# Another hand-written order for the seven step sequences of the second block's RWKV and convolution branch

## What is computed

```python
def conformer_conv(u, conv_w, conv_b, ln_g, ln_b):
    h = u[..., :D_CONV] * jax.nn.sigmoid(u[..., D_CONV:])
    h = lax.conv_general_dilated(h, conv_w[:, None, :], ..., feature_group_count=D_CONV) + conv_b  # 31 taps
    return jax.nn.silu(layer_norm(h, ln_g, ln_b))

def rwkv7_recurrence(r, w, k, v, kk, a):        # 8 heads of 64, one step a token
    def step(S, inp):
        s_kk = jnp.einsum("bhvk,bhk->bhv", S, kk_t)
        S = S * w_t - s_kk[..., None] * (kk_t * a_t) + v_t[..., None] * k_t
        return S, jnp.einsum("bhvk,bhk->bhv", S, r_t)
...
y = jnp.concatenate([y_conv, y_rwkv], axis=-1) @ w_out[i]
x = x + rms_norm(y, g[1])
```

## Time and profile before

| | us |
|---|---|
| median of 3 runs | 1634.03 |
| lowest, highest | 1633.18, 1635.67 |
| the profiled execution, its own time | 1632.09 |
| its span | 1630.2 |
| PE busy in the span | 1574.6 |
| first, second, third stretch (by windows) | 131.1, 118.7, 53.0 |

### The profile page before, as it was taken

One profiled execution on the slowest core, in us unless ns is written; L12 is line 12 of the kernel. 1 busy time (PEld: TensorE's weight loads), 2 busy tenths in 40 slices (PEclk: granted clock), 3 DMA queues, 4 the chain that ended last, 5 costly groups with the idle time before them and its releaser, 6 DMA issues.

```text
span 1630.2 us, 26875 instructions
## 1 busy us (share of the span) xinstructions
PE 1574.6 (97%) x11510; PEld 1298.0 (80%) x11510; DVE 819.4 (50%) x1243; ACT 604.0 (37%) x968; POOL 394.6 (24%) x326
## 2 busy tenths in 40 slices
PE   7999999999999999999999988899999999999997
PEld 7898778778888888888777767779779888888876
DVE  4777533446333333334679977547537332333334
ACT  4444322324323233244455544334345332232222
POOL 3111012022201011024057433023013430330234
PEclk9999999999999999999999988999999999999998
DMA  6325212223222323223321100032121222222211
GB/s 222 118 91 194 77 53 78 78 97 136 103 102 80 104 78 103 102 80 117 129 70 63 53 3 3 29 128 107 52 75 56 104 97 88 100 86 97 102 63 67
DMA packets 29221, 146.03 MB, mean 90 GB/s; under 512 B 3104, under 2 KB 6704, under 8 KB 14128
## 3 DMA queue, kind: packets, MB, share of 16 engines
q1 hardware_dynamic: 29104, 144.33, 24.9%
HBM read 138.03 MB, written 6.29 MB: 89 GB/s over the span
## 4 chain that ended last, share of the span: by engine, by line
PE 79%; DVE 9%; issue 7%; POOL 2%; ACT 2%; DMA 0%; SPq 0%; POOLq 0%; DVEq 0%
PE ps L170 78%; DVE zf L182 3%; DVE wl L182 2%; POOL zf L182 2%; DVE ps L190 1%; ACT zf L176 1%; DVE zf L190 1%; PE ps L173 1%; DVE zr L190 1%; DVE zf L2363 1%; ACT wh L179 0%; POOL tn L182 0%; DMA raw<-in_wstream 0%; ACT zr L179 0%; SPq L193 0%
## 5 line engine op out<-in xcount | busy, mean ns | idle before, releaser
L170 PE MATMUL ps<-zr,wh 128*128 128x512 f32 (+3 forms) x4048 | 1170.3, 376 | 9.9 <-ACT wh L179 5.7
L170 PEld LDWEIGHTS ps<-zr,wh 128*128 128x128 f32 (+1 forms) x4048 | 727.5, 189 | 157.9 <-ACT wh L179 5.7
L170 PE MATMUL ps<-zr,wl 128*128 128x512 f32 (+3 forms) x2024 | 748.6, 372 | 0.0
L182 POOL TENSOR_TENSOR zf<-zf 128x512 f32<-128x512 f32 (+1 forms) x237 | 286.6, 1215 | 765.0 <-ACT zf L176 505.5
L170 PEld LDWEIGHTS ps<-zr,wl 128*128 128x128 f32 (+1 forms) x2024 | 380.8, 189 | 71.7
L182 DVE TENSOR_TENSOR wl<-raw,wh 128x1024 fp32r<-128x1024 f32 (+1 forms) x244 | 305.8, 1292 | 204.2 <-ACT wh L179 204.1
L179 ACT ACTIVATE wh<-raw 128x1024 fp32r<-128x1024 f32 (+1 forms) x244 | 240.7, 1034 | 186.4 <-PE ps L170 185.2
L176 ACT ACTIVATE zf<-zf 128x512 f32<-128x512 f32 (+2 forms) x232 | 127.6, 561 | 370.6 <-DVE zf L182 257.7
L182 DVE TENSOR_TENSOR zf<-ps,zf 128x512 f32<-128x512 f32 (+4 forms) x172 | 98.0, 577 | 162.7 <-PE ps L170 140.8
L170 PE MATMUL ps<-zf 64*64 64x64 f32 (+6 forms) x3768 | 156.2, 247 | 20.9 <-issue 8.9
L170 PEld LDWEIGHTS ps<-zf 64*64 64x64 f32 (+3 forms) x3768 | 120.9, 150 | 59.2 <-issue 38.8
(11 more groups left out here) (81 smaller groups left out, 591.3 us busy)
## 6 DMA issues: line engine op xcount, KB each, us to landing
raw<-in_wstream SPq DMA_DIRECT2D x116, 1024.0 KB, 4.8
zf<-in_xT SPq DMA_DIRECT2D x16, 256.0 KB, 2.7
raw<-in_wstream SPq DMA_DIRECT2D x4, 768.0 KB, 4.4
kv_scratch<-zf SPq DMA_DIRECT2D x8, 256.0 KB, 2.2
x_scratch<-zf SPq DMA_DIRECT2D x8, 256.0 KB, 2.1
zf<-x_scratch SPq DMA_DIRECT2D x8, 256.0 KB, 4.8
out<-zf SPq DMA_DIRECT2D x16, 128.0 KB, 1.7
zf<-in_cu SPq DMA_DIRECT2D x1, 1256.0 KB, 8.9
```

Of the source, the lines that this page charges most:

```text
L170: return self.raw.matmul(out_, l, x, start=start, stop=stop)
L182: return self.raw.tensor_tensor(out_, a, b, o)
```

## The change

Only the 421 letters of `TURNS` differ; `TURNS_2`, all steps and all loops are the same. Every sequence advances as often as before; what changes is which letter stands where, and so how the steps lie between the half tiles and between each other.

```diff
 TURNS = """
-...ppp...pp.p.p.pp.pggggp.pppp.hhggg..ccgghhcccggg.hcccc..gcc.cggghghggghgccccgcc.hcccc.hcggggg.cc.hc.
+...ppp...pp.pp.p.pp..g.gpg.g.gpgcggg.pc.ccpcp.gg.hhccggcg.hgh.ggchch.ghccc.ghccggc.cgccch.hg.ghpppcc
```

More of the change, by code:

```diff
@@ L22 @@
 TURNS = """
[L23 to L27, removed]
+...ppp...pp.pp.p.pp..g.gpg.g.gpgcggg.pc.ccpcp.gg.hhccggcg.hgh.ggchch.ghccc.ghccggc.cgccch.hg.ghpppcc
+g.pgcch.cphgc.chchppcggg.cc.pggcp.hpcgghc.c.pgcp.hg.pcghc.gphcpiiphcggicipgigihccicffiggffpggccpcffc
+cifigifgpiccfpgiciifpfpcfgipifppicfpcpigcipfghifhchiphghppgfffhhcffccfhghfchcgfhpfchhgccccghfcpphfcp
+cfchpphhccfpppfhhppcifihfcihciciifficiifiicffifccoooioifiofiofifofoioifofoifioifffoffooffffofofofofo
+foofooofoooffoooooooo
 """
```

## The result

| us | before | changed |
|---|---|---|
| median of 20 runs | 1633.33 | 1635.32 |
| lowest, highest | 1628.84, 1635.67 | 1630.50, 1641.46 |
| ratio to before, 95% interval | 1 | 1.0019 (1.0010 to 1.0028) |
| profiled execution, its span | 1632.09, 1630.2 | 1634.29, 1632.5 |

The changed kernel is 0.19% slower, some 2 to 3 us, where 4.3 us less were forecast. The time lies in the stated range, the sign is wrong.

A forecast was written before the change was run, and what follows sets the result against it. TensorE, busy 97% of the span, was taken as the bound, so only its waits and half-clock time could be won. Terms -2.3 - 1.7 - 0.9 + 0.6 + 0 = -4.3 us gave 1629.7 against 1634.0, range 1624.5 to 1638.5.

The forecast's parts named there:

- (a): First stretch, third transpose of pair 0: four half tiles ahead of it hide the 2.32 us wait for VectorE, -2.3 us.
- (b): First stretch, behind that transpose: the 3.40 us half-clock window goes with the wait, -1.7 us.
- (c): First stretch, level 3 of pair 0: x 3 no longer waits 0.90 us for VectorE, -0.9 us.
- (d): New waits in the first stretch: only prep.kn 1 short of cover, at most 0.3 us, taken as 0.
- (e): More changes between dense and small steps, 82 instead of 74: four pairs more at 0.14 us, +0.6 us.
- (f): Second stretch: four more taps and new waits cost +3.2 us, fewer waits later repay; taken as 0, ends -5 and +9.5.
- a gain: Rival, second stretch: the 2.40 us wait, its half-clock window and state-step waits go, about -5 more, 1624.7 us; chance 0.20.
- given back: Rival: four waits behind the last p tile cost 3.2 us and nothing repays them, 1632.9 us; chance 0.20.
- Slower: the clock: Rival: waits within 14 us of the last p tile drop the clock, three more windows cost 9.5, 1639.2 us; chance 0.18.

The follow-up runs named there:

- y4_turn_heads: Kernel before with pair 0's third transpose behind one dense half and its first five head steps one or two half tiles later: 1630.50 us, 0.9975.
- e3_turn: Kernel before with only the third transpose of pair 0 and the gates of pair 1 one half tile later: 1637.24 us, 1.0018.
- x2_first_before: Order of the kernel before up to the last p tile, remaining letters behind it in the changed order: 1633.14 us, 1.0000 against before.
- y5_taps_late: Kernel before with four taps moved from the first stretch to behind the last p tile, nothing else: 1632.50 us, 0.9995.
- y1_level_back: Changed kernel with pair 0's last level put back ahead of the last dense half: 1634.23 us, 0.9998 against the kernel before.
- y2_level_late: Kernel before with x 5 and tz 4 of pair 0 moved behind the last dense half: 1637.15 us, 1.0022.
- a_look1: A further single trace of the changed kernel, nothing altered: 1639.12 us.
- z4_both: First stretch of z1_taps_off_level with the changed order behind the last p tile: 1631.72 us, 0.9993 against the kernel before.
- z1_taps_off_level: y4_turn_heads with two taps moved from ahead of level z 2 of pair 0 to behind x 3: 1631.40 us, 0.9984 against the kernel before.

## Why the prediction was wrong, step by step

(a) and (b) were right in mechanism and size: -2.3 and -1.7 at their place, in the changed kernel (no wait at the third transpose, granted clock 1.00 in the first stretch of all five traces) and alone in `y4_turn_heads` (-4.1 us by the ratio, -4.0 in its first stretch). `e3_turn` shows that the step behind the transpose needs cover as well; in the changed kernel the head steps come two half tiles behind it.

(c) was right at `x` 3 (between it and the `z` it needs stand a dense half and the gate product, no small step), but in the sum the new waits of (d) outweigh it.

(d) failed. I took 0 and bounded it by 0.3, after looking for steps with too little dense work between themselves and what they need. The changed kernel has four new waits in the first stretch: 1.05 us at `prep.gates` 1, and at `z` 1, `tz` 2 and `prep.vmm` 1:

```profile
860.86 0.67 PE L170 MATMUL ps<-zf 64*64 64x32 f32 x32 [0.37 <-DVE zf L182]
...
886.45 0.69 PE L170 MATMUL ps<-cf_sb,zf 64*64 64x64 f32 x32 [0.58 <-DVE zf L182]
899.02 1.10 PE L170 MATMUL ps<-zf,cf_sb 128*128 128x512 f32 x2 [0.53 <-DVE zf L190]
```

Together they are 2.5 us. All end on VectorE, whose queue there I had not walked. For the longest, these are VectorE's rows and then PE's:

```profile
870.13 3.12 DVE L190 SCALAR_TENSOR_TENSOR ps<-zf,vecs_sb,ps 128x512 f32<-128x512 f32 x4
873.16 3.44 DVE L182 TENSOR_TENSOR wl<-raw,wh 128x1024 fp32r<-128x1024 f32 x2
876.53 0.74 DVE L182 TENSOR_TENSOR zf<-ps,cu_sb 128x256 f32<-128x256 f32 x2
...
876.99 1.45 PE L170 MATMUL ps<-zf 64*128 64x512 f32 x4 [1.05 <-DVE zf L182]
```

`prep.gates` 1 takes the PSUM banks of `qt` 0, and VectorE empties them (876.53) only behind four taps and the split of a weight unit, 6.6 us of work. A dense half (2.8 us) between two steps is cover only if VectorE reaches its part within it, and a bank that comes round is a need like any other. With -4.9 for (a) to (c), +2.5 here, 59 records less (about -1.0) and the one pair of (e) that lies there (+0.1), the first stretch comes to -3.3 against -3.1 measured.

(e) can't be read by itself. Of its four pairs one lies in the first stretch and three in the third. PE is idle 0.4 us in the third, which takes 5.2 us more with 111 records that the other stretches have less; the 3 us named for them and three pairs of 0.14 were 1.8 too little. This is no loss of the whole by itself: `x2_first_before` has the same third stretch (58.0 us) and the time of the kernel before.

(f) failed, in its walk. VectorE's side of it held: the level was put at 5.1 us behind the last `p` tile and ended at 922.07 - 917.05 = 5.0. PE's side did not: I had PE "through at 4.8" and counted waits from `pk` on. PE was standing at `x` 5 and `tz` 4 for 1.53 and 1.75 us already, since each waits for VectorE's work on the step before it, so `pk` started at 9.5 instead of 6.5 and `fin.y` 0 at 36.0 instead of 31.6. The four taps, which I made the cause, cost nothing that the runs can tell from 0 (`y5_taps_late`); the level that lost its dense half costs 3.4 to 3.6 us (`y1_level_back`, `y2_level_late`), and it stood in the diff as two `h` less ahead of the last stop (19 for 21). What spoke for a gain, fewer waits at state steps and the 2.40 us wait, came in part (that wait is 0.70 and 1.58 us in two places now) and is worth nothing in the runs.

The sum as measured: -4.1 for (a) and (b), +2.5 less 0.9 for (d) and (c), +3.5 for the level, 0 for the second order: +1.0, where the runs give +2 to +3. Intervals of 1.6 to 2.6 us a term cover the difference. The traces show where it lies: up to `fin.y` 0 the five of the changed kernel take 36.0 to 40.0 us, 37.8 in the mean, for 31.7 before: +6.1, of which the first stretch gives back 3.1; behind `fin.y` 0 the means are 140.5 and 140.0. The trace with 36.0 has no half-clock window ahead of 940 us, the other four have; how much of the further 1.8 us is the clock's no run isolates.

The rivals: *given back* named the right outcome with the wrong cause. *Slower: the clock* was right in its mechanism, that waits within 14 us of the last `p` tile are followed by a fall of a clock that was full there (in six of the seven traces with the bare level), and the long runs lie at its 1639.2 (`a_look1` has its signs, 123.9 us in the second stretch and 41.0 at half clock). But the clock does not fall in each run, and the mean half-clock time of the two kernels is the same: by the means, the first stretch's 3.4 us went behind the last `p` tile. The Trainium skill, "TensorE: Matmul & The Clock Gate", section "What's actually happening", says that the window over which the gate judges activity runs free and is not reset when a kernel starts, so the point of a change varies. The traces agree: five of one kernel have five patterns behind the last `p` tile, while PE's waits at `x` 5 and `tz` 4 repeat to 0.01 (1.53 or 1.54, and 1.75). So a single trace's windows should not be added up as a property of a kernel, as I did in (f).

## What to carry to other kernels

Where an in-order engine alternates dense blocks with short chains through a second engine, the last chain ahead of the end of the dense blocks needs its cover most: count how many of its steps stand ahead of the last block before and after a reorder, and walk both engines in turn, since each wait of one moves the other. A step moved past a wait takes its followers on all engines with it (here a copy behind a weight split), so move the consumers too. Half the length of a throttled window is its price in dense work (1.6 us for 3.4, below); among short steps that wait for other engines take the price from the runs.

## What the runs showed of the hardware

A us at half clock went with 0.16 to 0.36 us of time over the runs of the two kernels. Why it is less than 0.5 is not shown; 27.3 us of it in the first trace of before lie in the second stretch, where steps are short and often wait for another engine anyway. In the dense part it is near 0.5: `z4_both` and `z1_taps_off_level` have the same first stretch with the same 1.6 us of idleness, and it takes 129.3 us with one window of 3.4 us for 127.7 without. The same wait need not bring such a window: behind 1.57 and 1.56 us at `prep.norm` 1 the clock stays full in `z1_taps_off_level` and falls in `z4_both`, both at 887.3 among dense matmuls, 28 records against 10 in 3.4 us. `z1_taps_off_level`, then `z4_both`:

```profile
887.30:890.70 3.40, 3.40 (x28) 2.61 (x26) 3.37 (x6) 2.79 (x4) 3.40 (x3) 1.00 0.00 0
```

```profile
887.30:890.70 3.40, 3.40 (x10) 2.63 (x9) 3.37 (x5) 2.79 (x4) 3.40 (x3) 0.50 0.00 0
```

The waits for "issue" stayed: 6.6 us in 8 waits for 8.5 in 9, in another order of the same steps. Each stands 126 or 127 records, or a multiple of that, behind the one before it: 253, 630, 126, 253, 126, 757, 126 and 127 before, and 127, 126, 883, 126, 127, 880 and 127 in the changed kernel. So they go by the count of records and not by the steps, and an order of the table can't be expected to win them.
